# A two-layer hybrid decoder on 8 cores: half of the pool inputs after the convolution inputs, two convolution blocks inside the recurrence, the tail in pairs, SSM copies of the FFN stage one step later

## The reference

```python
h = rms_norm(x, norm1); z = h @ w_in                      # (B, S, 5120)
u_a, v_b, u_c, gates = split(z)                           # 512, 1024, 512, 3 x 1024
y_a = s5_mixer(u_a, ...) @ ssm_w_proj                     # complex diagonal recurrence, state 64, 32 groups; gelu; GLU
y_b = conv_module(v_b, ...)                               # a * sigmoid(b), causal depthwise conv of 31 taps, LayerNorm, silu, w_proj
y_c = pool_mixer(u_c, ...)                                # causal means over 2, 4, 8, 16 positions minus u, grouped matmul, w_proj
x = x + (gates[0] * y_a + gates[1] * y_b + gates[2] * y_c) @ w_out
h = rms_norm(x, norm2); x = x + (silu(h @ w_gate) * (h @ w_up)) @ w_down     # hidden size 2816
```

## Time and profile before

| | us |
|---|---|
| median of 3 runs | 2108.72 (2107.98 to 2110.8) |
| profiled execution, its own time | 2113.91 |
| span of its slowest core | 2112.4 |
| spans of the eight cores | 2100.7 to 2112.4 |
| TensorE busy | 1981.5 |
| VectorE busy | 1012.3 |
| ScalarE busy | 669.2 |

### The profile page before, as it was taken

How to read it: one execution, slowest core, us unless ns; L and a number is a source line. 1 busy time by engine, 2 the same in 40 slices (tenths; PEclk the granted TensorE clock), 3 DMA queues, 4 the chain that set the end, 5 groups by cost and what they waited for, 6 DMA issues and landing times.

```text
span 2112.4 us, 30921 instructions; the slowest of 8 cores (2100.7 to 2112.4 us)
## 1 busy us (share of the span) xinstructions
PE 1981.5 (94%) x11354; PEld 921.5 (44%) x11536; DVE 1012.3 (48%) x1484; ACT 669.2 (32%) x1106; POOL 85.1 (4%) x160
## 2 busy tenths in 40 slices
PE   3887999999999998999997998999999999999997
PEld 1433634444444443444443454444444444444443
DVE  6789464444454444342263865544446223233136
ACT  6632572222333203223242246522224210110123
POOL 1000000000000000000000000000000000000000
PEclk9999999999999999999998999999999999999999
DMA  9533543122422222343266464221133120312203
GB/s 244 104 81 59 95 71 73 21 40 40 139 51 51 60 34 47 61 74 76 70 183 140 100 126 74 68 41 29 32 88 110 32 40 11 70 31 41 40 11 160
DMA packets 56371, 154.21 MB, mean 73 GB/s; under 512 B 5920, under 2 KB 26784, under 8 KB 53408
## 3 DMA queue, kind: packets, MB, share of 16 engines
q0 software_dynamic: 21456, 77.05, 21.8%
q1 hardware_dynamic: 31888, 72.03, 11.0%
q10 hardware_dynamic: 2880, 3.15, 0.6%
HBM read 189.39 MB, written 25.17 MB: 102 GB/s over the span
## 4 chain that ended last, share of the span: by engine, by line
PE 84%; DVE 6%; issue 4%; ACT 4%; DMA 1%; ACTq 0%; DVEq 0%
PE ps L254 84%; DVE tmp L224 1%; DVE gt L224 1%; ACT sq_s L243 1%; DVE h L232 1%; DMA ud<-stg 1%; DVE cv L224 0%; DVE tmp L830 0%; ACT yb L243 0%; ACTq L270 0%; ACT wc L243 0%; DVE stg L232 0%; DVE bp L224 0%; DVE hprev L224 0%; ACT g L243 0%
## 5 line engine op out<-in xcount | busy, mean ns | idle before, releaser
L254 PE MATMUL ps<-h,slot 128*128 128x512 bf16 x5261 | 1201.1, 381 | 34.4 <-DVE stg L232 12.6
L254 PEld LDWEIGHTS ps<-h,slot 128*128 128x128 bf16 x5376 | 526.3, 98 | 666.1 <-issue 48.4
L224 DVE TENSOR_TENSOR actb<-ps,sgf 128x512 bf16<-128x512 f32 x176 | 121.6, 692 | 429.3 <-PE ps L254 398.2
L254 PE MATMUL ps<-actb,slot 128*128 128x512 bf16 x1378 | 304.1, 379 | 1.6
L243 ACT ACTIVATE sgf<-ps 128x512 f32<-128x512 f32 x176 | 104.9, 596 | 583.8 <-PE ps L254 574.5
L232 DVE SCALAR_TENSOR_TENSOR acc<-gt,ps 128x512 f32<-128x512 f32 x180 | 123.5, 688 | 238.8 <-PE ps L254 234.5
L243 ACT ACTIVATE gt<-ps,hb 128x512 f32<-128x512 f32 x192 | 130.6, 686 | 330.4 <-PE ps L254 330.4
L254 PEld LDWEIGHTS ps<-actb,slot 128*128 128x128 bf16 x1408 | 137.7, 98 | 165.9
L224 DVE TENSOR_TENSOR x<-ps,x 128x512 f32<-128x512 f32 x192 | 130.3, 690 | 134.1 <-PE ps L254 134.0
L261 POOL DMA_DIRECT2D slot<-wts x146 | 77.1, 531 | 1875.2 <-PE ps L254 1835.8
L254 PE MATMUL ps<-mg,slot 128*128 128x512 bf16 x502 | 114.7, 387 | 6.1 <-DVE mg L232 5.6
(11 more groups left out here) (129 smaller groups left out, 1202.2 us busy)
## 6 DMA issues: line engine op xcount, KB each, us to landing
slot<-wts POOLq DMA_DIRECT2D x146, 512.0 KB, 6.3
x<-xT SPq DMA_DIRECT2D x16, 512.0 KB, 17.6
x<-xT SPq DMA_DIRECT2D x4, 2048.0 KB, 16.8
x_mid<-x SPq DMA_DIRECT2D x4, 2048.0 KB, 8.2
x<-x_mid SPq DMA_DIRECT2D x4, 2048.0 KB, 16.8
outT<-x SPq DMA_DIRECT2D x4, 2048.0 KB, 6.4
uc<-stg SPq DMA_DIRECT2D x64, 64.0 KB, 2.7
hc<-stg SPq DMA_DIRECT2D x32, 128.0 KB, 2.9
```

The lines of the kernel that those rows point to most:

```text
L224: return (eng or dve).put(lambda e: e.tensor_tensor(out=out, in0=a, in1=b, op=op), after)
L254: ins = e.matmul(out, lhsT=a, rhs=b, start=start and i == 0, stop=stop and i == n - 1, **kw)
```

## The change

Seven edits, all of order or placement; one moves four operations to another engine.

1. The slots load the two pool weights a second time, after those of the convolution inputs (75 loads a layer for 73). Pool blocks 0 and 1 are computed first, then all convolution blocks, then pool blocks 2 and 3, which stage in STG 2 and 3.
2. In the recurrence, `scan` has 16 pieces for 20 (two short scans in one), st1 of the next group comes after piece 8, and fewer pieces stand beside each projection (two for four in layer 0, two for three in layer 1). In layer 0 it begins one block earlier, and the generator is stepped faster before it. The first HC spreads wait until the generator has ended (`hc_spread`).
3. `conv(0)` and `conv(1)` are generators now and stand inside the recurrence, beside its last pieces; pool_edge comes after them.
4. The tail alternates: pool_sums(0), st2(0), pool_sums(1), st2(1), and so on, with the LayerNorm of blocks 0 and 1 between. KM is loaded in halves.
5. The squares of convolution blocks 2 and 3 are taken by ScalarE (four operations) in place of VectorE (one).
6. In layer 1 three of the four w loads (W1) wait for the last ud spread, and st1(0) comes after both pool blocks.
7. In `gens(1)` a pause (`yield`) stands before each pair of wc copies and before each `inside`; kst has two buffers. In layer 0 the four kst tiles lie where STG 0 and 1 do, not where TG does.

```diff
-    order = u + p + c + cd[:7] + [("glu", 0)] + cd[7:] + [("wpc", 0), ("wpc", 1)]
+    order = u + p + c + p + cd[:7] + [("glu", 0)] + cd[7:] + [("wpc", 0), ("wpc", 1)]
...
-    KSTS = [[at("kst%d" % i, [4, 2, 128], BF16, o_x + 40960 + 2048 * (i % 3)) for i in range(4)],
-            [at("kst", [4, 2, 128], BF16, o_rb + 8192)] * 4]
+    KSTS = [[at("kst%d" % i, [4, 2, 128], BF16, o_x + 2048 * i) for i in range(4)],
+            [at("kst1_%d" % i, [4, 2, 128], BF16, o_rb + 8192 + 2048 * i) for i in range(2)] * 2]
...
@@ out_mats @@
                 free[1] = td
+                if l:
+                    yield
                 for g in range(2):
...
@@ inside @@
+            if l:
+                yield
             dst = KSTS[l][pt][:, :]
-            kb = lay["x_free"][2] + (k_all[pt - 3] if pt > 2 else []) if l == 0 else begin
+            kb = begin + (k_all[pt - 2] if pt > 1 else []) if l else lay["kst_free"]
...
@@ p_blk, c_blk @@
-            k = 4 + b % 2
+            k = 4 + b if b < 2 else b
...
-                if b == NB - 1 and m % 2:
+                if b % 2 and m % 2:
                     give_back(n, t)
...
-            S["hc"].append(spread(b, k, HC, tv + S["re_free"]))
+            S["hc_wait"].append((b, k, tv))
+            if S["re_free"] is not None:
+                hc_spread()
...
@@ scan @@
-                    yield
+                    if q4 % 2:
+                        yield
...
@@ st2 @@
-            after = [bank_free[i] for i in bs] + S["hprev"][2 * pt:2 * pt + 2] + S["km"] + S["ud"] + out["wc"]
+            after = [bank_free[i] for i in bs] + S["hprev"][2 * pt:2 * pt + 2] + [S["km"][pt // 2]] + S["ud"] + out["wc"]
...
@@ ln_sum @@
-            S["sq"][b] = tt(CSQ[b % 2][:, :], cv[:, :], cv[:, :], ALU.mult, tc + [S["csq_free"][b % 2], S["tmp_free"]])
+            if b < 2:
+                S["sq"][b] = [tt(CSQ[b % 2][:, :], cv[:, :], cv[:, :], ALU.mult, tc + [S["csq_free"][b % 2], S["tmp_free"]])]
+                return
+            S["sq"][b] = [actv(CSQ[b % 2][:, r], cv[:, r], AF.Square, tc + [S["csq_free"][b % 2], S["tmp_free"]]) for r in range(4)]
...
@@ ssm @@
-                    if i == 12 and pt < 3:
+                    if i == 8 and pt < 3:
                         st1(pt + 1)
-                    if i > 4 and i % 2 == 0:
+                    if i > 3:
                         step(S["rots"])
...
@@ layer 0 @@
-            for k, _ in enumerate(all_of(p_blk)):
-                step(g0, 1)
-                if k == 7:
+            lay["kst_free"] = S["stg_free"][0] + S["stg_free"][1]
+            S["hp_free"] = lambda pt: out["k"] if pt < 2 else S["stg_free"][pt + 2]
+            for k, _ in enumerate(some_of(p_blk, (0, 1))):
+                step(g0, 1 if k > 4 else 2)
+                if k == 4:
                     turn["from"] = [4, 5, 6, 7]
-                if k >= 7:
+                if k > 4:
                     step(sc, 2)
...
+            S["re_free"] = None
+            for k, _ in enumerate(some_of(c_blk, range(NB))):
                 step(g0, 2)
+                step(sc, 2)
                 want_tabs()
-                step(sc, 4)
-                if k == 5:
-                    pool_edge()
-            drain(g0)
+                if k == 6:
+                    drain(g0)
+                    S["re_free"] = out["re"]
+                    S["pads"].append(mset(pool, HC[:, :, :, 0:4], 0.0, S["re_free"]))
+                    hc_spread()
+            S["ws_p"] = [slot(l, "p", c) for c in range(2)]
+            for _ in some_of(p_blk, (2, 3)):
+                step(sc, 2)
...
@@ layer 1 @@
+            def w1_load(pt):
+                S["w1"].append([dma(sp, W1[:, 4 * pt:4 * pt + 4], s_w1[:, 4 * pt:4 * pt + 4], d_w1l[pt],
+                                    lay["rb_free"] + out["w1"] + (S["ud"][-1:] if pt else []))])
+            S["w1"] = []
+            w1_load(0)
             for b in range(1, NB):
                 drain(u_blk(b))
+            for pt in range(1, 4):
+                w1_load(pt)
...
-            for k, _ in enumerate(all_of(p_blk)):
-                if k > 3:
-                    step(sc, 2)
-                    want_tabs()
-            for _ in all_of(c_blk):
-                step(sc, 3)
+            for _ in some_of(p_blk, (0, 1)):
+                pass
+            for _ in some_of(c_blk, range(NB)):
+                step(sc, 2)
                 want_tabs()
-            pool_edge()
+            S["ws_p"] = [slot(l, "p", c) for c in range(2)]
+            for _ in some_of(p_blk, (2, 3)):
+                step(sc, 1)
...
@@ both layers @@
+        for h in range(2):
+            q = slice(8 * h, 8 * h + 8)
+            S["km"].append(dma(sp, KM[:, q], s_k[:, q], d_kl[h], S["x2_free"] + out["k"] + S["stg_free"][2 + h]))
...
+        while S["sums"] < 2:
+            step(sc)
+        for _ in conv_by(0):
+            step(sc, 2)
+        while S["sums"] < 4:
+            step(sc)
+        for _ in conv_by(1):
+            step(sc, 2)
+        pool_edge()
         drain(sc)
...
-        for m in range(4):
-            pool_sums(m)
-        conv(0)
+        pool_sums(0)
         ln_sum(0)
-        conv(1)
+        st2(0)
         ln_sum(1)
-        st2(0)
+        pool_sums(1)
+        st2(1)
         ln_stat(0)
-        st2(1)
+        pool_sums(2)
         ln_stat(1)
         ln_rs(0)
         ln_rs(1)
         ln_apply(0)
+        st2(2)
+        pool_sums(3)
+        st2(3)
         ln_apply(1)
-        st2(2)
-        st2(3)
         conv(2)
+        ln_sum(2)
```

49 lines of the change are left out of this document (24 added, 25 removed).

## The result

| | before | after |
|---|---|---|
| median of 17 runs each, us | 2110.8 | 2080.4 |
| profiled execution, its own time | 2113.91 | 2080.31 |
| span of its slowest core | 2112.4 | 2078.7 |
| spans of its eight cores | 2100.7 to 2112.4 | 2073.9 to 2078.7 |
| median of these spans | 2104.0 | 2076.9 |

The ratio of after to before is 0.9867, 95% interval 0.9848 to 0.9885, so the change is 24 to 32 us faster. The prediction was 2074, with a range of 2062 to 2092. It is 2075.9 for the change, and 2104.5 to 2105.1 for the kernel before.

What follows compares the result with a forecast made beforehand. TensorE, busy 94% of the span, was taken as the bound, so only its idle or half-rate time counts. First layer 12.0, FFN 10.5, second layer 12.0: 34.5 us, giving 2074 us against the 2108.72 median; range 2062 to 2092.

Steps and rivals of the forecast that it cites:

- Layer 0, stg waits: First layer's recurrence: two steps between projections for four make TensorE the bound; stg waits go, 25.2 us together.
- first rival: The new wait's bank chain holds TensorE through the c projections, so the first layer gives nothing: 2086 us; 12%.
- new wait at st1(0): First layer: st1(0) waits 7.9 us until kst is read out; with half rate and bank waits, 10.6 us come back.
- fifth rival: The change does all it says and the wait at st1(0) is short: 7 us more, 2067 us; 14%.
- Nothing is charged: First layer: VectorE's recurrence ends at 213 us, before TensorE needs its LayerNorm sums; no cost, margin only 3 us.
- Convolution blocks as cover for the end of the recurrence: Two convolution blocks, some 7.9 us each on TensorE, stand beside the recurrence's left-over VectorE steps.
- Tail in pairs: Both layers: alternating pool_sums and st2 waits for evacuations, 4.4 us against 2.5; with moved squares, 2.6 us lost per layer.
- fourth rival: No evacuation in the tail is hidden: 19 us a layer, 2108 us, over 2113 with a late recurrence; 6%.
- FFN: First layer's FFN: wc copies right behind the VectorE work they need remove sgf waits and half rate; 10.5 us won.
- Head of layer 1: Second layer's head: later w loads and st1(0) remove ud and stg waits; 14.6 us, less 2.6 for the tail: 12.0.
- Table loads: Tail: Exp between Gelu and tanh may add two table loads per layer, 2.6 us of ScalarE; no cost counted.
- third rival: Each table switch stops ScalarE for twice 1.28 us, and both tails lose 2.5 us more: 2079 us; 3%.

Runs made afterwards that it cites:

- e11: e8's kernel with banks 0 to 3 kept free two projections earlier in layer 0, and slots held in layer 1 too: 2074.78 us at best, median core 2070.2.
- e8: Changed kernel, layer 0's four slots freed by conv(0) and conv(1) asked for again only behind pool_edge: 2070.38 us at best, median core 2067.9, ratio to before 0.9806.
- e13: e8's kernel run again, beside the unaltered changed kernel: 2092.15 us, ratio to before 0.9798, median core 2066.4.
- e14: The changed kernel unaltered, run again as comparison for e13: 2096.01 us, ratio to before 0.9816, median core 2075.4.
- e7: Changed kernel with the recurrence drained before conv(0) and conv(1) in the program's text: 2079.46 us median, median core 2075.8.
- e12: Changed kernel with layer 1's projection order undone (pool blocks 2 and 3 ahead of convolution inputs, old staging buffers): 2100.86 us, ratio 0.9896, median core 2094.9.
- e6: Changed kernel with the tail's order of the kernel before (all four pool_sums first): 2084.82 us at best, median core 2076.0.
- e1: Kernel before plus the FFN part alone (pauses before wc copies and each inside, two kst buffers): ratio 0.9965, median core 2092.6.
- e4: Changed kernel with pool blocks 2 and 3 ahead of convolution block 3 in layer 0: 2110.32 us, ratio 0.9991.
- e2: Kernel before plus three w loads deferred behind the last ud spread, st1(0) left in place: 2104.46 us, median core 2098.5.
- e3: Changed kernel with all four w loads ahead of the ud spreads again, st1(0) left late: 2085.45 us, median core 2076.1.

## Why the prediction was right, and where it was not

The direction, the size and the range held: 2074 forecast, 2080.4 measured, against a kernel before that took 2110.8 in these runs rather than the 2108.72 that the forecast started from (2.1 us of the 6.4 that are missing). For the profiled execution the forecast was 2079.4 and the measurement 2080.31. That closeness is in part luck: on the slowest core the term of layer 0 was too large by 6.0 us and that of layer 1 too small by 5.5.

- **Layer 0, stg waits: right.** Two steps between the projections made TensorE the bound there. From 128 us to pool_edge TensorE waits for nothing, so the first rival falls; the 9.4 us missing from 100 to 128 us are the st1(0) wait and two stg waits.
- **Layer 0, new wait at st1(0): right, a little smaller.** TensorE got there at 98.7 us (predicted 99.1) and waited 6.5 us and 0.4 (7.9). The fifth rival (a short wait) falls with it. The prediction had kst hold the banks; by the trace it is ScalarE's stg, which stands between wc copies that wait for VectorE, and kst only for the last 0.4 us. e11 bears this out so far that keeping other banks free moves the wait and does not remove it. The two bank waits behind it cost 3.7 us, 1 was counted.
- **Layer 0, "Nothing is charged" for the way to pool_sums(0): wrong.** This is the step that failed. TensorE reached that place at 210.4 us, near the predicted 209. VectorE ended the recurrence later than predicted (216.5 us, and 218.1 in e8, for 213) but was in time (e8's rows above). But only VectorE's sums were asked about, not what else pool_edge and pool_sums read. UC's last transfer had 7 us to land, since half of the pool inputs now come last, and the slots that the moved convolution blocks give back were loaded beside it. The text did ask whether the doubled pool weights had time to land, and left out which transfers the new loads would slow. It cost 8.3 us and the half rate behind it, 9.4 in all (e8; 8.5 in e13 against e14). With it the layer gains 5.7 us for 12.0; without it, 15.1. The list of signs "Wrong would be" had waits on hc and slots and not on uc. Of those it had, the one on a slot did come, with about 1 us at the start of each Merge on half of the cores.
- **Convolution blocks as cover for the end of the recurrence: not tested.** e7's queues are those of the change, so it says nothing on this. What was shown, in layer 1, is that the order of c and the second half of p counts for another reason than VectorE's: it covers the landing of the last HC spread (e12).
- **Tail in pairs: a cost of 2.6 us a layer was counted; no such cost shows.** In layer 0 the waits for evacuations are 2.08, 0.40 and 0.78 us, 3.3 in all for the 4.4 counted, against 1.68 and 0.40 in the kernel before (2.5 counted). Beside these, the kernel before waits 2.9 us for edge in pool_sums and 1.6 for the evictions inside `fold` (wpr), and both are gone; the prediction had not listed them. Inside the changed kernel the order is worth 0.1 to 0.7 us at the median core (e6). The fourth rival falls with it.
- **FFN: right**, 10.5 counted, 10.5 alone (e1) and 11.4 within the change.
- **Head of layer 1: right in kind, mis-sized.** The ud and stg waits went on all eight cores, the issue takes 2.80 us for 9.55. On the profiled slowest core layer 1 gained 17.5 us, on the median core 9.8; 12.0 was forecast. The rows were those of the core that had these waits longest (10.4 us of waits for stg and ud; the other seven had 6.9 to 8.1), and the run's time is that of the slowest core. So much of the gain is that this core came down to the others: the cores' spans lay 11.7 us apart before and 4.8 after.
- **Table loads: right.** Two more loads in the program (34 for 32), one a layer where two were allowed for. In the tail of layer 0 ScalarE's next operation again starts 1.30 us after the load does, so the third rival falls, and the extra drain that the Trainium skill (ScalarE: Activation LUTs, What ACT_TABLE_LOAD costs) names does not show here:

```profile
226.47 1.28 ACT L243 ACT_TABLE_LOAD   x1 [2.41 <-PE ps L254]
227.77 2.06 ACT L243 ACTIVATE g<-ps 128x512 bf16<-128x512 f32 x4
```

The version of e8 beats both kernels: 2070.4 us at best and 2067.9 at the median core, where the change has 2078.5 and 2075.9.

## What to carry to other kernels

When a stage is moved, ask of the first consumer behind it not only which engine it waits for but which transfer, how long ago it was issued, and what else the queues carry then; a moved stage takes its buffer releases with it, and these start loads that compete with the transfers of its new neighbours. Holding back loads that nobody needs yet (here four slots, by 4 to 14 us) gave 8 to 9 us net in layer 0; the same in layer 1, where TensorE waits for up to 2.5 us at pool_edge, gave nothing (e11). Before an experiment on order is read, look whether the queue of any engine changed: moving calls past each other in the text moves nothing when they belong to different engines (e7). Size a gain from the slowest core's rows only for that core, and look at the others too: what is left is how far the slowest stands out.

## What the hardware showed that was not expected

- A spread out of SBUF into SBUF (16 transfers of 64 KB, or 4 of 128 KB) lands in 2.1 to 3 us at its quickest. The slowest took 15.9 us (uc in the change, beside six slot loads of 512 KB), 12.9 us (hc in e4, beside four slot loads and the two of KM) and 12.8 us (uc at the head of layer 1 in e8, behind the w loads and beside two slot loads). The last of layer 0's sixteen uc transfers was issued by 203.5 us in the change and had landed at 218.6, 15 us later; in e8 it was issued by 205.6 and had landed by 211.8, within 6.2 us. Why a few transfers wait so long while most land in 6 to 8 us stays open.
- Issuing a DMA can hold the issuing engine: four issues on ScalarE's queue took 2.6 us or 7.9 to 9.6 us, by whether 1.5 MB of loads were queued ahead on another queue (2.55 in e2; 9.55 before, 8.10 in e1, 7.91 in e3). Two issues of KM on SyncE's queue took 12.94 us in the change and 2.15 in e8, where four slot loads of GpSimd's queue are gone from that time.
- One and the same wait was followed by different clocks on different cores (e6, layer 1). TensorE waits 2.77 us for lt (2.86 on core 6), and from there to the wait for g the same matmuls run at a granted clock of 1.00 on core 3 (8.3 us), 0.82 to 0.84 on cores 2, 4, 5 and 7 (9.2 to 9.6 us) and 0.70 to 0.71 on cores 0, 1 and 6 (11.5 to 11.6 us). Cores 0, 1 and 6 also wait longest for csq (1.0 to 1.4 us), but core 3 waits 1.0 us for it too and keeps its clock. What decides was not tried.
